# Bias tables of an attention block: reversed by TensorE, or loaded ready from repeated rows in DRAM

## The chip, the core and the metric

One NeuronCore of a Trainium2 chip runs the whole program; no other core takes part. The metric is the device time of one execution in microseconds (us). Engines are named TensorE (PE, with its weight load PEld), VectorE (DVE), ScalarE (ACT) and SyncE (SP), which here only issues DMAs. GpSimd does nothing.

## The reference

Two blocks in a row, for 256 tokens of width 1024, all in float32. The first has two layers; each is: a SwiGLU feed-forward (inner width 2816), a projection to three attention branches, the branches themselves, a gated merge, and a second feed-forward. The second block mixes attention and retention and ends in a mixture of experts; the change does not touch it. What matters here are the additive tables of the three branches:

```python
# neighbourhood branch, 8 heads, tokens on a grid of 4 rows x 64 columns
dr = row_idx - r[:, None] + (NA_WIN_ROWS - 1)
dc = jnp.clip(c[None, :] - c[:, None] + (NA_WIN_COLS - 1), 0, 2 * NA_WIN_COLS - 2)
bias = rpb[:, dr[:, None, :, None], dc[None, :, None, :]]
logits = jnp.where(col_ok[:, None, :], logits + bias, NEG_INF)
# differential and windowed branch, 4 + 8 heads
rel = kpos[None, :] - (start + qoff)[:, None]
bias = bias_table[t5_bucket(rel)]
```

Both tables depend only on key position minus query position. So each row of a table is the row above it, moved by one element. The neighbourhood table differs between the layers; the T5 table is the same for both.

## The kernel before, in words

**Weights.** All weights pass through a stream of pieces of 512 KB (`stream_plan`, `stream`), issued by SP in one fixed order into six buffers `W`. A piece i may be issued when piece i - 6 has been used up. Most pieces are split into two parts that TensorE multiplies at full rate: ScalarE rounds a piece to its high part (`halves`, L1324), VectorE subtracts to get the low part (`rests`, L1663), and four pairs of such parts (`WH`, `WL`) are kept. A product is then three matmuls. In one feed-forward, block b (of 11) takes two pieces for the gate, two for the up product and two for the down product of block b - 1, so 66 pieces in all; then the projection takes 30.

**Order.** Each engine runs its own list in order; semaphores tie them. TensorE's results go to four work banks of PSUM in turn (`begin`, `turns`), so a bank must be emptied four turns later. VectorE and ScalarE take the splits of the next pieces ahead of the emptying of a bank (`used`, then `take`), so a late piece holds both up.

**Bias rows.** Early in the first feed-forward the kernel makes the 112 padded rows of the neighbourhood bias (16 heads of both layers x 7 rows of 128) and 12 rows of 512 for T5, and stores them to the DRAM scratch `na_scr` and `t5_scr` (`store_bias_rows`). A DMA then reads a row once for each partition, one element further on each time (`load_t5` into `R5`, `load_na` and `load_na_bias` into `R`, which lies over `QK`). [...] TensorE turns it round by a product with the reversed identity `anti` (`bias`, recorded at L652 as reading R or QK, and C), and VectorE empties the bank into `T5` (L1810) or adds the column mask and writes `Z` (L1813). `bias_tables` deals three tables to each block from block 3 on: 12 + 8 in the first feed-forward of layer 0, 8 in that of layer 1. The loads of layer 0 stand in SP's stream at pieces 23, 28 and 33; those of layer 1 are issued by ScalarE between the norm and the second feed-forward of layer 0 (L1410).

**AdaLN units.** 24 products for the second block's modulation are dealt to chosen blocks (`ADA_BLOCKS`). Their weights have two buffers; the first four units use only the first of them, since `R5` takes the place of the other, and SP waits for the buffer ahead of a block's gate pieces (`load_ada`, L543).

## Time and profile before

| | us |
|---|---|
| runs, median (lowest to highest) | 2165.75 (2164.09 to 2170.45) |
| the profiled execution: its own time | 2166.41 |
| its span, from the first to the last instruction | 2164.6 |
| TensorE busy | 2062.4 |
| VectorE busy | 1181.1 |
| ScalarE busy | 637.2 |
| mean granted TensorE clock, share of full | 0.983 |

The profile is one execution; times in it count from the start of its span. A matmul's listed duration contains the depth of the pipeline, and matmuls overlap, so what one costs is the distance between starts. "Idle before" an instruction names what released it. SPq and ACTq are the DMA-issuing instructions of SP and ScalarE; a long one waited for room in its queue. q1 is SP's DMA queue, q10 ScalarE's. The names QK, T and t_scr in rows are the program's, numbers left out: T is `T5`, R is `R5`. The four feed-forwards start at about 18, 527, 731 and 1235 us.

### The profile page before, as it was taken

Reading aid. Unit: us, or ns where it says so; the run is one execution under the profiler, and the core shown is the slowest. Engines: PE = TensorE matmul, PEld = TensorE weight load, DVE = VectorE, ACT = ScalarE, POOL = GpSimd, SP = SyncE. Lnnn points to the kernel's source line nnn. Section 1 sums busy time; section 2 is a strip of 40 time slices with the busy share of each in tenths; the row PEclk is TensorE's granted clock in tenths of the full one; section 3 lists DMA queues with packets and bytes.
Section 4 is the critical chain, followed back from the end, with each engine's and each line's share of the span. In section 5 each row is a group of like instructions: output and inputs, shape, how many; then the busy total and the mean of one; then the engine's idle time right before and its main releaser. Section 6 shows DMA issues by size and latency. Waiting matters only on the chain.

```text
span 2164.6 us, 33353 instructions
## 1 busy us (share of the span) xinstructions
PE 2062.4 (95%) x14055; PEld 1676.9 (77%) x14055; DVE 1181.1 (55%) x2009; ACT 637.2 (29%) x942; POOL 0.2 (0%) x4
## 2 busy tenths in 40 slices
PE   7999999999999999999998999979997999999997
PEld 7999998878999999999886899978765543444443
DVE  6665659773656666565987365565275422222222
ACT  4433434432433533343443243320042000000001
POOL 0000000000000000000000000000000000000000
PEclk9999999999999999999999999999989999999999
DMA  7976563226966676556322677632224799999996
GB/s 226 276 218 178 164 184 98 88 88 193 282 216 201 200 225 216 176 158 185 103 92 78 195 243 215 195 73 78 79 97 175 315 422 420 421 421 421 421 421 252
DMA packets 260676, 471.39 MB, mean 218 GB/s; under 512 B 15418, under 2 KB 221300, under 8 KB 235948
## 3 DMA queue, kind: packets, MB, share of 16 engines
q1 hardware_dynamic: 259216, 466.25, 62.8%
q10 hardware_dynamic: 1308, 2.96, 0.6%
q8 instruction: 114, 1.87, 0.4%
q14 instruction: 38, 0.31, 0.0%
HBM read 468.03 MB, written 1.13 MB: 217 GB/s over the span
## 4 chain that ended last, share of the span: by engine, by line
PE 77%; DMA 17%; DVE 4%; ACT 1%; issue 1%; SPq 0%; DVEq 0%; ACTq 0%
PE ps L652 75%; DMA ring_zone<-in_moe_w_up_dram 15%; DMA W<-in_ffn_w_gate_dram 2%; PE ps L937 1%; DVE QK L1949 1%; PE ps L1082 0%; DVE hl L1674 0%; DVE WL L1663 0%; DVE xT L1681 0%; ACT WH L1324 0%; DMA PT<-in_norm_g_dram 0%; SPq L581 0%; DVE xT L1726 0%; DVE yT L1952 0%; DVE xT L1861 0%
## 5 line engine op out<-in xcount | busy, mean ns | idle before, releaser
L1663 DVE TENSOR_TENSOR WL<-W,WH 128x1024 fp32r<-128x1024 f32 x372 | 453.0, 1223 | 337.7 <-ACT WH L1324 337.7
L652 PE MATMUL ps<-hh,WH 128*128 128x256 f32 x2128 | 608.0, 286 | 13.4 <-DVE WL L1663 7.7
L652 PE MATMUL ps<-hl,WH 128*128 128x256 f32 x2128 | 598.1, 281 | 0.0
L652 PE MATMUL ps<-hh,WL 128*128 128x256 f32 x2128 | 597.9, 281 | 0.0
L1324 ACT ACTIVATE WH<-W 128x1024 fp32r<-128x1024 f32 x372 | 391.5, 1056 | 486.3 <-PE ps L652 455.9
L652 PEld LDWEIGHTS ps<-hh,WH 128*128 128x128 f32 x2128 | 404.0, 190 | 34.0 <-issue 31.1
L652 PEld LDWEIGHTS ps<-hl,WH 128*128 128x128 f32 x2128 | 404.1, 190 | 0.2
L652 PEld LDWEIGHTS ps<-hh,WL 128*128 128x128 f32 x2128 | 403.7, 190 | 0.0
L652 PE MATMUL ps<-ring_over,XT 128*64 128x512 f32 x896 | 228.4, 595 | 30.2 <-DMA ring_zone<-in_moe_w_up_dram 13.6
L652 PEld LDWEIGHTS ps<-ring_over,XT 128*64 128x64 f32 x896 | 77.7, 137 | 174.9 <-issue 174.5
L652 PE MATMUL ps<-hid_h,WH 128*128 128x256 f32 x704 | 201.7, 287 | 0.0
L652 PE MATMUL ps<-hid_l,WH 128*128 128x256 f32 x704 | 197.0, 280 | 0.0
L652 PE MATMUL ps<-hid_h,WL 128*128 128x256 f32 x704 | 196.8, 280 | 0.0
L1596 ACT ACTIVATE sgE<-ps 128x512 f32<-128x512 f32 x16 | 9.6, 597 | 447.5 <-PE ps L652 447.5
L652 PEld LDWEIGHTS ps<-hid_h,WH 128*128 128x128 f32 x704 | 132.6, 188 | 6.3 <-issue 5.8
L652 PEld LDWEIGHTS ps<-hid_l,WH 128*128 128x128 f32 x704 | 132.7, 188 | 0.5
L652 PEld LDWEIGHTS ps<-hid_h,WL 128*128 128x128 f32 x704 | 132.5, 188 | 0.0
L2379 DVE TENSOR_TENSOR hidE<-sgE,ps 128x512 f32<-128x512 f32 x16 | 16.8, 1048 | 205.0 <-PE ps L652 205.0
L652 PE MATMUL ps<-yT,W 128*128 128x256 f32 x512 | 116.7, 381 | 0.0
L652 PE MATMUL ps<-ring_zone,hidT 128*64 128x512 f32 x512 | 113.4, 595 | 0.8 <-DVE SelT L2361 0.7
L652 PEld LDWEIGHTS ps<-yT,W 128*128 128x128 f32 x512 | 95.0, 190 | 15.0 <-issue 3.6
L652 PEld LDWEIGHTS ps<-ring_zone,hidT 128*64 128x64 f32 x512 | 37.8, 137 | 65.4 <-issue 64.0
(336 smaller groups left out, 2343.5 us busy)
## 6 DMA issues: line engine op xcount, KB each, us to landing
ring_over<-in_moe_w_gate_dram SPq DMA_DIRECT2D x64, 1024.0 KB, 20.3
ring_zone<-in_moe_w_down_dram SPq DMA_DIRECT2D x64, 1024.0 KB, 18.9
ring_over<-in_moe_w_up_dram SPq DMA_DIRECT2D x48, 1024.0 KB, 22.3
W<-in_ffn_w_gate_dram SPq DMA_DIRECT2D x88, 512.0 KB, 5.2
W<-in_ffn_w_up_dram SPq DMA_DIRECT2D x88, 512.0 KB, 4.4
W<-in_ffn_w_down_dram SPq DMA_DIRECT2D x88, 512.0 KB, 4.2
W<-in_w_in_dram SPq DMA_DIRECT2D x78, 512.0 KB, 4.0
W<-in_w_gate_dram SPq DMA_DIRECT2D x48, 512.0 KB, 3.6
```

Source lines behind the costliest of these rows:

```text
L652: ins = nc.tensor.matmul(o, lhsT, rhs, start=start, stop=stop, skip_group_check=True, **kw)
L937: ins = nc.tensor.transpose(bank[:, k * T + q * P:k * T + (q + 1) * P], S[:, u % 4, q * T + k * P:q * T + (k + 1) * P], ident)
L1324: nc.scalar.activation(high, W[:, i % RAW, :], ACT.Copy).then_inc(high_ready, 1)
L1596: nc.scalar.activation(sgE[:, :], bank, ACT.Silu).then_inc(sg_ready, 1)
L1663: v.tensor_tensor(low, W[:, i % RAW, :], high.bitcast(F32), ALU.subtract).then_inc(low_ready, 1)
L1949: give(v.reciprocal(r2, r2))
L2379: v.tensor_tensor(hidE[:, :].rearrange("p (k m) -> p m k", k=HIDDEN), by_row(sgE[:, :]), by_row(bank), ALU.mult).then_inc(work_free, 2)
```

## The change

The rows go to DRAM scratch as before, and from there once more: each T5 row is copied 128 times in a row into `t5_rep` (12 x 128 x 512), each head's seven neighbourhood rows 64 times into `na_rep` (16 x 64 x 896), by two DMAs from DRAM to DRAM whose source repeats. In such a scratch a partition can read its own copy of the row one element further back than the partition before it (its start moves on by 511 or 895 elements), so the tables arrive in their right order: T5 straight in `T5` by one DMA of 128 x 12 runs of 1536 B, the neighbourhood table straight in `Z` by 16 DMAs (8 heads, two halves of 64 partitions) of 64 x 6 runs of 256 B each. The products, their work-bank turns and their evictions go; the column mask is added in place by VectorE during the projection (steps 2 to 9). SP issues the copies at pieces 36 and 42, waits for both before the T5 load at piece 50, and issues the 16 loads of layer 0 at piece 56; ScalarE issues the 16 of layer 1 where it issued two. VectorE waits for the T5 table ahead of the first projection, and for the neighbourhood table at its step 2. With `R` and `R5` gone, both adaLN buffers lie over `QK` and alternate from the first unit on.

The diff, cut (calls of `bias` and `bias_tables` in the engines' lists are left out):

```diff
@@ -28,7 +28,7 @@
-NA_RUN = 5 * P + 64
+NA_ROW = NA_ROWS * P
@@ -134,7 +133,7 @@
 def ada_buffer(u):
-    return 0 if u < ADA_ALONE else u % 2
+    return u % 2
 def ada_loads(u):
@@ -149,16 +148,8 @@
-STORE_AT, T5_AT, NA_AT = 20, 23, (28, 33)
-def bias_tables(l, i, b):
-    if i or not 3 <= b < FF_BLOCKS:
-        return []
-    tables = [("t5", h) for h in range(12)] + [("na", h) for h in range(NA_H)]
-    at = 3 * (b - 3)
-    return [t for t in tables[at:at + 3] if l == 0 or t[0] == "na"]
+STORE_AT, REPEAT_AT, T5_AT, NA_AT = 20, (36, 42), 50, 56
+NA_SHIFTS = 64
 def stream_plan():
@@ -304,12 +295,9 @@
-        _, R5, ada_a = zone(("V_and_QK", [P, TT * 1152 + 22 * T], F32), ("R5", [P, 12, 3 * P], F32),
-                            ("ada_a", [P, 2, PIECE], F32))
-        ada_b = zone(("up_to_ada_b", [P, TT * 1152 + 22 * T + 12 * 3 * P - 2 * PIECE], F32),
-                     ("ada_b", [P, 2, PIECE], F32))[1]
+        _, ada_a, ada_b = zone(("V_only", [P, TT * 1152], F32), ("ada_a", [P, 2, PIECE], F32),
+                               ("ada_b", [P, 2, PIECE], F32))
...
-        R5 = R5[:, :, :]
@@ -328,7 +316,6 @@
-        R = flat(QK[:, :, :]).rearrange("p (h n) -> p h n", h=NA_H)
@@ -371,6 +358,19 @@
+        na_rep = nc.dram_tensor("na_rep", (DEPTH * NA_H, NA_SHIFTS, NA_ROW), F32, kind="Internal").ap()
+        t5_rep = nc.dram_tensor("t5_rep", (12, P, 512), F32, kind="Internal").ap()
+        def load_na(queue, l):
+            for half in range(2):
+                first = l * NA_H * NA_SHIFTS * NA_ROW + (1 - half) * P + NA_SHIFTS - 1
+                for h in range(NA_H):
+                    src = bass.AP(tensor=na_rep.tensor, offset=first + h * NA_SHIFTS * NA_ROW,
+                                  ap=[[NA_ROW - 1, NA_SHIFTS], [P, 6], [1, 64]])
+                    queue.dma_start(Z[half * 64:half * 64 + 64, h, :].rearrange("p (a n) -> p a n", a=6), src)\
+                        .then_inc(r_load, 16)
@@ -598,16 +599,16 @@
                 sp.wait_ge(t5r, due(t5r))
...
+            def repeat_rows(scratch, rows, n):
+                return bass.AP(tensor=scratch.tensor, offset=0, ap=[[n, rows.shape[0]], [0, rows.shape[1]], [1, n]])
             def load_t5():
-                sp.wait_ge(scr, due(scr, 32))
-                src = bass.AP(tensor=t5_scr.tensor, offset=0, ap=[[1, P], [512, 12], [1, 3 * P]])
-                sp.dma_start(R5, src).then_inc(t5_load, 16)
-            def load_na(half):
-                src = bass.AP(tensor=na_scr.tensor, offset=half * P, ap=[[1, 64], [NA_ROWS * P, NA_H], [1, NA_RUN]])
-                sp.dma_start(R[half * 64:half * 64 + 64, :, :], src).then_inc(r_load, 16)
+                sp.wait_ge(repeated, 32)
+                sp.wait_ge(setup, 2)
+                src = bass.AP(tensor=t5_rep.tensor, offset=P - 1, ap=[[511, P], [P * 512, 12], [1, 3 * P]])
+                sp.dma_start(T5[:, :, :], src).then_inc(t5_load, 16)
             stream(0, RAW)
@@ -617,13 +618,16 @@
             stream(RAW, STORE_AT)
...
-            stream(STORE_AT, T5_AT)
+            stream(STORE_AT, REPEAT_AT[0])
+            sp.wait_ge(scr, due(scr, 32))
+            sp.dma_start(t5_rep, repeat_rows(t5_scr, t5_rep, 512)).then_inc(repeated, 16)
+            stream(REPEAT_AT[0], REPEAT_AT[1])
+            sp.dma_start(na_rep, repeat_rows(na_scr, na_rep, NA_ROW)).then_inc(repeated, 16)
+            stream(REPEAT_AT[1], T5_AT)
...
-            stream(T5_AT, NA_AT[0])
-            load_na(0)
-            stream(NA_AT[0], NA_AT[1])
-            load_na(1)
-            stream(NA_AT[1], moe_at)
+            stream(T5_AT, NA_AT)
+            load_na(sp, 0)
+            stream(NA_AT, moe_at)
...
             sp.wait_ge(table_ready, 1)
@@ -748,22 +752,6 @@
                 for tt in range(TT):
...
-            def bias(l, i, b):
-                for kind, h in bias_tables(l, i, b):
-                    if h == 0 and kind == "t5":
-                        pe.wait_ge(t5_load, 16)
-                    if h == 0 and kind == "na":
-                        pe.wait_ge(r_load, 32 * (l + 1))
-                    bank = begin()
-                    if kind == "t5":
-                        mm(bank[:, 0:384], anti, R5[:, h, :], True, True, then=work_ready)
-                    else:
-                        src = R[:, h, 0:640].rearrange("p (a n) -> p a n", n=P)[:, :, 0:64]
-                        mm(bank[:, 0:320], anti, src, True, True)
-                        mm(bank[:, 320:384], anti, R[:, h, 640:704], True, True, then=work_ready)
-                    turns.step()
             def norm():
@@ -1396,18 +1383,10 @@
                     if (l, i, b) == (0, 0, LATE_BLOCK):
...
-                    turns.step(len(bias_tables(l, i, b)))
                     if b:
...
-            def load_na_bias(l):
-                for half in range(2):
-                    first = (l * NA_H * NA_ROWS + half) * P
-                    src = bass.AP(tensor=na_scr.tensor, offset=first, ap=[[1, 64], [NA_ROWS * P, NA_H], [1, NA_RUN]])
-                    act.dma_start(R[half * 64:half * 64 + 64, :, :], src).then_inc(r_load, 16)
             def rows(tile, at, n, src):
@@ -1482,7 +1461,7 @@
                 if l + 1 < DEPTH:
-                    load_na_bias(l + 1)
+                    load_na(act, l + 1)
@@ -1802,16 +1781,13 @@
-            def bias(l, i, b):
-                for kind, h in bias_tables(l, i, b):
-                    bank = take()
-                    if kind == "t5":
-                        give(v.tensor_copy(T5[:, h, :], bank[:, 0:384]))
-                    else:
-                        mask = const("na_mask").rearrange("p (a n) -> p a n", a=1).to_broadcast([P, 6, 64])
-                        give(v.tensor_tensor(Z[:, h, :].rearrange("p (a n) -> p a n", a=6),
-                                             bank[:, 0:384].rearrange("p (a n) -> p a n", a=6), mask, ALU.add))
+            def mask_columns(l, h):
+                if h == 0:
+                    dve.wait_ge(r_load, 16 * 2 * NA_H * (l + 1))
+                mask = const("na_mask").rearrange("p (a n) -> p a n", a=1).to_broadcast([P, 6, 64])
+                z = Z[:, h, :].rearrange("p (a n) -> p a n", a=6)
+                return v.tensor_tensor(z, z, mask, ALU.add)
             def ffn(l, i):
                 for b in range(FF_BLOCKS):
@@ -1839,7 +1815,6 @@
                     if ada_unit(l, i, b - 1) is not None:
...
-                    bias(l, i, b)
                     if b:
...
                 if ada_unit(l, i, FF_BLOCKS - 1) is not None:
@@ -1868,7 +1843,11 @@
             for l in range(DEPTH):
...
+                if l == 0:
+                    dve.wait_ge(t5_load, 16)
                 for c in range(15):
+                    if 2 <= c < 2 + NA_H:
+                        link(mask_columns(l, c - 2))
                     if c != 1:
...
                     if c == 0:
```

## Rows read from the trace of the kernel before

**Rows 1.** page, parts 1 and 4: busy us; the chain by engine
```profile
PE 2062.4 (95%) x14055; PEld 1676.9 (77%) x14055; DVE 1181.1 (55%) x2009; ACT 637.2 (29%) x942; POOL 0.2 (0%) x4
...
PE 77%; DMA 17%; DVE 4%; ACT 1%; issue 1%; SPq 0%; DVEq 0%; ACTq 0%
```

**Rows 2.** timeline of TensorE, blocks 3 and 7: start us, us, engine, line, operation
```profile
77.43 0.29 PE L652 MATMUL ps<-hh,WL 128*128 128x256 f32 x1
77.55 2.10 PE L652 MATMUL ps<-R,C 128*128 128x384 f32 x6
...
79.61 0.28 PE L652 MATMUL ps<-hid_l,WH 128*128 128x256 f32 x1
...
158.05 2.48 PE L652 MATMUL ps<-QK,C 128*128 128x320 f32 x12
...
160.53 0.28 PE L652 MATMUL ps<-hid_l,WH 128*128 128x256 f32 x1
```

**Rows 3.** waits, whole span: us in total, times, longest
```profile
ACT WH L1324 <- PE ps L652: 455.9, 248, 5.4
```

**Rows 4.** timeline of TensorE, block 5, in brackets the idle time before
```profile
116.74 1.54 PE L652 MATMUL ps<-R,C 128*128 128x384 f32 x4
120.20 0.91 PE L652 MATMUL ps<-R,C 128*128 128x384 f32 x2 [1.92 <-DVE S L1827]
```

**Rows 5.** the chain in order of time, 60 to 235 us
```profile
100.86 16.35 DMA W<-in_ffn_w_gate_dram
```

**Rows 6.** waits of SP's own queue, 90 to 101 us
```profile
SPq L543 <- PE ps L652: 4.0, 1, 4.0
```

**Rows 7.** waits of TensorE, 520 to 600 us
```profile
PE ps L652 <- DVE WL L1663: 2.1, 2, 1.2
```

**Rows 8.** groups by line: busy us, mean ns of one | idle before
```profile
L1813 DVE TENSOR_TENSOR Z<-ps,C 128x384 f32<-128x384 f32 x16 | 8.0, 549 | 0.1
```

**Rows 9.** windows, projection: busy us by engine, PEclk, DMA share, GB/s
```profile
250.00:270.00 20.00, 20.00 (x171) 19.86 (x170) 13.49 (x17) 6.92 (x8) 0.00 (x0) 1.00 0.63 184
```

**Rows 10.** timeline of SP: pieces 36 and 37, pieces 56 and 57
```profile
110.36 4.14 SPq L581 DMA_DIRECT2D W<-in_ffn_w_up_dram  x2
...
171.54 4.21 SPq L581 DMA_DIRECT2D W<-in_ffn_w_down_dram  x2
```

**Rows 11.** DMA issues, whole span: KB each, median us to landing
```profile
W<-in_ffn_w_gate_dram SPq DMA_DIRECT2D x88, 512.0 KB, 5.2
...
R<-t_scr SPq DMA_DIRECT2D x1, 2304.0 KB, 14.1
```

**Rows 12.** windows: small packets; loads into 64 partitions beside weights
```profile
18.50:21.00 2.50, 2.50 (x15) 2.50 (x15) 1.23 (x1) 0.00 (x0) 0.00 (x0) 0.61 1.21 84
...
80.00:94.00 14.00, 14.00 (x122) 14.00 (x121) 8.78 (x17) 5.69 (x6) 0.00 (x0) 1.00 1.06 260
```

**Rows 13.** DMA packets, 18.5 to 21 us, then 72 to 76 us
```profile
DMA packets 2376, 0.21 MB, mean 84 GB/s; under 512 B 2341, under 2 KB 2372, under 8 KB 2376
...
DMA packets 1103, 1.48 MB, mean 370 GB/s; under 512 B 15, under 2 KB 1102, under 8 KB 1102
```

**Rows 14.** timeline of ScalarE and its queue at the loads of layer 1
```profile
528.62 0.73 ACTq L1410 DMA_DIRECT2D QK<-na_scr  x1
...
529.42 2.18 ACT L1343 ACTIVATE mT<-xT 128x512 f32<-128x512 f32 x4
531.50 1.99 ACT L1324 ACTIVATE WH<-W 128x1024 fp32r<-128x1024 f32 x2
```

**Rows 15.** timeline of TensorE, second feed-forward, start of the up product
```profile
534.38 0.38 PE L652 MATMUL ps<-hh,WH 128*128 128x256 f32 x1
```

**Rows 16.** timeline of SP, one weight piece
```profile
535.24 9.44 SPq L581 DMA_DIRECT2D W<-in_ffn_w_gate_dram  x1
```

**Rows 17.** DMA queues, 530 to 543 us: packets, MB, share of 16 engines
```profile
q10 hardware_dynamic: 655, 1.80, 58.2%
q1 hardware_dynamic: 1530, 1.66, 48.8%
```

More of the change, by code:

```diff
@@ L122 @@
               ((1, 1), (1, 3, 4, 6, 7, 9)))
-ADA_ALONE = 4
 ADA_UNITS = {}
@@ L419, in build @@
         scr = ev("scratch_written")
+        repeated = ev("scratch_repeated")
         r_load = ev("shifted_load")
@@ L1841, in ffn @@
                         ada_columns(ada_unit(l, i, b - 1))
-                    bias(l, i, b)
                     if b:
```

## The prediction

> **What bounds the kernel now.** Read first the busy shares and the chain of waits [rows 1]: TensorE is busy for 95% of the span and carries 77% of the chain; the DMA share of 17% belongs almost wholly to the expert stage, which the change doesn't touch. So in the feed-forward stages an instruction taken off TensorE should shorten the span by what it held TensorE for, and VectorE (55%) and ScalarE (29%) count only where they make TensorE wait. Next the order of TensorE's instructions around the bias products [rows 2]: an ordinary product (listed at 0.29 us, which is pipeline depth) is followed 0.12 us after its start, so cost has to be read from starts, not from durations. Then the two places in these stages where TensorE stood still [rows 4, 7] and what was late there. Last the rates of the DMA engines and how two queues share them [rows 12, 13, 17], because the change trades products for transfers.
>
> **Removed: 28 bias products.** In block 3 of the first feed-forward the step before the products starts at 77.43, the three T5 products at 77.55, and the second ordinary product after them at 79.61; without them it would start at 77.67. Three T5 products (the six instructions of the row) cost 1.94 us, and the twelve of them stand in four blocks: 7.8 us. Three neighbourhood products (twelve instructions) run from 158.05, and the second ordinary product starts at 160.53 where 158.17 would do: 2.36 us, 0.79 each. There are 16, eight in each layer: 12.6 us. Together 20.4 us off TensorE, and nothing lies beside them: over the kernel ScalarE waits 455.9 us for TensorE before its roundings, 248 times [rows 3], so the work on weights follows TensorE and not the other way round.
>
> **Removed: two stalls.** The first is inside block 5: the third product starts at 120.20, after a wait of 1.92 us, where 116.74 and two thirds of 1.94 make 118.03, so 2.2 us are lost [rows 4]. Its chain is a weight piece issued at 100.86 that took 16.35 us to land behind two skewed neighbourhood loads [rows 5]; SP had also stood 4.0 us for the single adaLN buffer before it [rows 6]. From the moment the piece could have gone to its landing is 16.35 + 4.0 + 1 for the adaLN issues, some 21 us, and 2.2 us of that reached TensorE. So some 19 us of lateness of a piece are covered: this is the cover I use below. Both causes go: the loads move, and the first four adaLN units now alternate. The second stall is 2.1 us at 558 to 564 [rows 7], a piece late behind the second layer's loads (2.9 MB). They become 1.6 MB. I take both as gone, unless something of the new takes their place: 4.3 us.
>
> **Moved on VectorE.** 28 evictions leave the feed-forward, and 16 mask additions, which took 0.55 us each out of PSUM [rows 8], enter the input projection, reading SBUF now. There VectorE is busy 13.5 of 20 us while TensorE is busy for all 20 [rows 9], so an addition of about that length in each of 8 steps hides. Bounds: 0 to 16 x 0.6 = 10 us if each held up an eviction that TensorE waits for; I take 0.3, by the idle third. The new wait for the T5 table stands at the end of the stage; its load is issued 16 pieces before that end. A piece takes 3.06 us (piece 36 at 110.36, piece 56 at 171.54 [rows 10]), so 49 us earlier, and the load took 14.1 us in its old form [rows 11]. The neighbourhood table is issued 10 pieces before the end and wanted two projection steps of some 5.6 us after it, 42 us in all. Neither is late; queued behind these waits on VectorE would be the low halves of all weights.
>
> **Added: two copies from DRAM to DRAM**, 3.1 MB and 3.7 MB, on SP's queue at pieces 36 and 42, that is about 107 and 125 us [rows 10]. The trace of before shows no such transfer. At the saturated rate of 370 GB/s [rows 13] they take 8.5 and 10 us; if a byte read and written in DRAM counts twice, 17 and 20. A piece behind them lands that much after its usual 5.2 us [rows 11]. Against 19 us of cover the first case costs 0, the second 3 + 6 = 9 us. I take 1, since loads into SBUF run at that rate and the copies lie 18 us apart. SP's wait for both comes at piece 50, about 150 us: 25 us after the second, hidden in the first case, some us late in the second (in the 9).
>
> **Added: the tables' own loads.** The T5 load is the same 2.3 MB as before. The neighbourhood table becomes 16 transfers of 384 runs of 256 B, 6144 runs for a layer, instead of 2 of 512 long ones. Price of a run: between 18.5 and 21 us the engines moved 2376 packets, 2341 of them under 512 B, in 2.5 us, the engines full (share 1.21) [rows 12, 13]: 1.05 ns each over 16 engines, so 6.5 us. From above, packets of 1.3 KB took 4 us for 1103 [rows 13], 3.6 ns each, so 22 us. I take 1.5 ns, near the row with packets of their size.
>
> In layer 0, SP issues them at piece 56, about 170 us. An issue took up to 0.73 us on ScalarE for 512 runs [rows 14], so SP is held 16 times that at most, 12 us, and the piece behind lands inside the 19 us. At 3.6 ns it would be 22 + 5.2 - 19 = 8.5 us late. I take 1.
>
> In layer 1, ScalarE issues them, and this is the dear place. At 528.6 it issues two now; the four squares already handed over run until 531.6, and the next weight piece is rounded at 531.50 [rows 14]. Queued behind the sixteen issues are these roundings (with the low halves on VectorE behind them), the sum's copy and the square root. TensorE has three pieces in hand and starts the up projection at 534.38 [rows 15]; the fourth piece is needed 24 products later, at 537.2. Rounding (1.06), low half (1.22) and handshakes take 2.4 us, so ScalarE must be free by 534.8, 6.2 us after the first issue. Sixteen issues at 0.73 with nothing else end at 540.3: 5.5 us lost. At half that, nothing. A queue also fills: with five pieces of 512 runs ahead, one issue took 9.44 us [rows 16], so about 2560 runs fit and 3584 must drain first, in half of the engines' time, as the two queues share them now (58% and 49%) [rows 17]. At 1.05 ns that is 7.5 us (1.3 lost), at 1.5 ns 10.8 (4.6), at 3.6 ns 25.8 (19.6). I take 6.
>
> The Trainium skill (DMA: Bandwidth & Descriptors, Specifications) has a rule against this change: under 512 B a DMA engine reads, modifies and writes, so full rate needs at least that. If a run of 256 B costs like one of 512 B, a layer's table takes 8.5 us at 370 GB/s, 1.4 ns a run, close to what the small-packet row allows; the sum would not move.
>
> **Sum**, against the profiled execution (2166.4 us, its span 2164.6): -20.4 - 4.3 + 0.3 + 1 + 1 + 6 = -16.4, so 2150.0. That execution lies 0.7 us above the median of the three runs (2165.75), inside their spread (2164.09 to 2170.45); I say 2150.
>
> **The rivals.**
> *A, part of the gain comes back in the small loads*, 2 to 3 ns a run: ScalarE is held 14 to 21 us (8 to 15 lost), SP's piece is late by 0 to 5, the copies take 1 to 2. With the 25 us gained: 2153 to 2163, say 2160. For it: loads into 64 partitions ran at 260 GB/s [rows 12] where others ran at 370 [rows 13], and the new ones write 64 partitions too. Against: the packets of their size were cheap.
> *B, slower than before.* The same mechanism with its upper price at each place: 19.6 on ScalarE, 8.5 on SP, 9 at the copies, 0.3 on VectorE, against 24.7: +12.7, 2179. With p the price of a run in ns and 2 us for the copies, the loss is (7.17p - 6.2) + (6.14p - 13.8) + 2, and passes 24.7 at p = 3.2. That needs small packets to cost three times what they did at 20 us.
> *C, the products were hidden anyway*, so that the blocks are paced by the splitting of weights and only the stalls go: about 2164. Against it stand ScalarE's waits for TensorE [rows 3] and the gapless starts around the products [rows 2].
> *D, everything is covered*: ScalarE is free in time and nothing is late: 2166.4 - 24.7 = 2142.
>
> **Chances.** Forecast 0.62 (its own range 2145 to 2156), A 0.15, B 0.08, C 0.05, D 0.10. What a measurement can tell from no change is 0.3%, 6.5 us, so the line is 2159.3: faster 0.62 + 0.10 + half of A = 0.80; within it half of A and C, 0.12; slower 0.08. The range 2142 to 2163 leaves out B and edges of C and D.
>
> **What would show it.** TensorE: no rows from the reversing matrix, and each block with three of them shorter by 1.9 to 2.4 us; the layer-1 gap at 534 to 540, released by the low half of a weight, of about 6 us; no gap at 118 or 560. ScalarE: sixteen issues of 0.4 to 0.8 us each; if later ones take over 1 us, the queue filled and A is at work. SP: an idle stretch before the T5 load means that the copies were dear. The forecast is wrong if the blocks do not shorten by these amounts, if TensorE stands still in the first layer between 110 and 200 us for over 3 us, or if VectorE waits for a table.

## The result, and the profile after

| | before | after |
|---|---|---|
| runs, median (lowest to highest), us | 2166.04 (2164.09 to 2170.45) | 2148.09 (2148.00 to 2150.22) |
| ratio, 95% interval | | 0.9917 (0.9899 to 0.9934) |
| span of the profiled execution, us | 2164.6 | 2148.4 |

Faster by 0.8%, where 2150 was forecast. In a later session, beside other runs of before, the same kernel stood at 0.9937 (0.9918 to 0.9956).

The page of the kernel after, parts 1, 2 and 4: busy us by engine, packets of the DMA engines, the chain by engine, to be held against [rows 1].

```profile
PE 2042.2 (95%) x13967; PEld 1660.9 (77%) x13967; DVE 1175.9 (55%) x1997; ACT 637.0 (30%) x942; POOL 0.2 (0%) x4
...
DMA packets 273951, 475.57 MB, mean 221 GB/s; under 512 B 28182, under 2 KB 234064, under 8 KB 249224
...
PE 78%; DMA 15%; DVE 4%; ACT 1%; ACTq 1%; issue 0%; SPq 0%; DVEq 0%
```

TensorE lost 88 instructions and 20.2 us of busy time, which are the 28 groups of products. The chain lost two points of DMA (the late pieces), and ACTq, ScalarE's DMA issues, rose in it from 0% to 1%. The gain by stage is read best from windows that are cut at the same instructions in every kernel, at VectorE's `hl` in the norms that stand before and behind a feed-forward; FFN(l,i) is feed-forward i of layer l. The columns are the window, its length, busy us by engine, PEclk, DMA share, GB/s. Before: attention of layer 0, FFN(0,1), FFN(1,0).

```profile
230.19:528.49 298.30, 291.57 (x1929) 255.76 (x1930) 202.46 (x388) 110.86 (x216) 0.00 (x0) 0.99 0.42 128
528.49:729.33 200.84, 197.84 (x1737) 191.50 (x1735) 122.94 (x145) 82.41 (x89) 0.00 (x0) 1.00 0.78 234
729.33:935.98 206.65, 204.74 (x1774) 197.29 (x1774) 128.46 (x158) 84.21 (x94) 0.00 (x0) 1.00 0.65 199
```

The same stages of the kernel after.

```profile
214.62:513.01 298.39, 291.66 (x1929) 255.54 (x1930) 206.35 (x395) 110.86 (x216) 0.00 (x0) 0.99 0.42 129
513.01:721.21 208.20, 199.64 (x1737) 193.45 (x1735) 122.91 (x144) 82.15 (x89) 0.00 (x0) 0.98 0.76 219
721.21:921.65 200.44, 198.54 (x1742) 192.38 (x1742) 124.64 (x149) 84.25 (x94) 0.00 (x0) 1.00 0.68 205
```

FFN(0,0) ends at 214.62 instead of 230.19: 15.6 us gained. Attention is unchanged. FFN(0,1) is 7.4 us longer. FFN(1,0) is 6.2 us shorter. Behind it 1.8 us are gained (1228.6 to 1226.8), where the change only adds the mask additions of layer 1: 1.6 of them fall in layer 1's projection and attention, whose first 20 us ran at a granted clock of 0.91 before and 1.00 after. Windows of 2 us at the same place, 4.0 us into that stage, before and then after:

```profile
939.98:941.98 2.00, 2.00 (x11) 2.00 (x11) 0.45 (x2) 2.00 (x5) 0.00 (x0) 0.50 0.00 0
```

```profile
925.65:927.65 2.00, 2.00 (x20) 2.00 (x19) 0.46 (x2) 2.00 (x5) 0.00 (x0) 1.00 0.04 8
```

In both, TensorE had stopped for the same 1.54 us in the norm ahead of them. All stages together give -16.2, as the spans do.

The loss is one gap. TensorE and ScalarE of the kernel after around it (start us, us, operation, in brackets the idle time before):

```profile
529.62 0.58 PE L656 MATMUL ps<-hh,WH 128*128 128x256 f32 x1 [7.65 <-DVE WL L1642]
```

```profile
513.14 0.73 ACTq L371 DMA_DIRECT2D Z<-na_rep  x1
...
515.99 11.15 ACTq L371 DMA_DIRECT2D Z<-na_rep  x12
527.25 2.95 ACT L1311 ACTIVATE WH<-W 128x1024 fp32r<-128x1024 f32 x3 [11.13 <-issue]
```

From the first issue at 513.14 to the end of the last at 527.15 ScalarE was held for 14.0 us, and the next weight piece could be rounded only then. The chain of waits shows the single issues; these are four of them, from 517 to 523 us (start us, us, what):

```profile
517.63 2.03 ACTq L371
...
519.69 0.65 ACTq L371
...
520.37 2.04 ACTq L371
...
522.44 0.65 ACTq L371
```

Two of the sixteen took 2.0 us and one 0.91; the last seven took 0.65 each. And the gap costs more than its length. Windows of the kernel after behind it: PEclk is the third column from the right.

```profile
525.00:529.00 4.00, 0.00 (x0) 0.00 (x0) 0.66 (x1) 1.75 (x2) 0.00 (x0) 0.67 1.40 153
529.00:531.00 2.00, 1.38 (x6) 1.38 (x7) 2.00 (x3) 1.91 (x3) 0.00 (x0) 0.50 0.92 121
531.00:533.00 2.00, 2.00 (x12) 2.00 (x11) 1.97 (x2) 1.91 (x3) 0.00 (x0) 0.50 0.88 310
533.00:535.00 2.00, 2.00 (x16) 1.95 (x16) 0.00 (x0) 0.23 (x1) 0.00 (x0) 0.95 1.08 370
```

For the first 3.6 us after the gap TensorE ran at half of full clock (1.2 instead of 2.4 GHz), a matmul every 0.21 us instead of every 0.12: some 1.7 us more. The Trainium skill (TensorE: Matmul & The Clock Gate, Part 1) says that an idle array falls back to the lower of its two clocks; the trace agrees, 0.50 behind an idle stretch of 7.65 us.

### The profile page after: what moved, and what is told of

It reads as the page before. It is cut to its first block, busy times and chain, and to the rows that moved or that the text cites. A ratio compares the mean times of both kernels' runs of the same rounds, so it can differ in the third digit from the quotient of the medians.

```text
span 2148.4 us, 33210 instructions
## 1 busy us (share of the span) xinstructions
PE 2042.2 (95%) x13967; PEld 1660.9 (77%) x13967; DVE 1175.9 (55%) x1997; ACT 637.0 (30%) x942; POOL 0.2 (0%) x4
## 4 chain that ended last, share of the span: by engine, by line
PE 78%; DMA 15%; DVE 4%; ACT 1%; ACTq 1%; issue 0%; SPq 0%; DVEq 0%
PE ps L656 77%; DMA ring_zone<-in_moe_w_up_dram 15%; PE ps L924 1%; DVE QK L1928 1%; ACTq L371 1%; PE ps L1069 0%; DVE hl L1653 0%; DVE xT L1660 0%; DVE WL L1642 0%; DMA PT<-in_norm_g_dram 0%; SPq L582 0%; ACT WH L1311 0%; DVE xT L1705 0%; DVE yT L1931 0%; DVE xT L1836 0%
## 6 DMA issues: line engine op xcount, KB each, us to landing
ring_over<-in_moe_w_gate_dram SPq DMA_DIRECT2D x64, 1024.0 KB, 20.4
```

## The experiments

All stage times are those windows. "Wait" is TensorE's wait behind ScalarE's issues in FFN(0,1), "hold" the time from ScalarE's first such issue to the end of its last.

| kernel | median us | ratio to before (95%) | FFN(0,0) ends | FFN(0,1) | FFN(1,0) | hold | wait |
|---|---|---|---|---|---|---|---|
| before | 2162.4 to 2166.0 | 1 | 230.19 | 200.84 | 206.65 | | |
| after | 2148.09 | 0.9917 (0.9899 to 0.9934) | 214.62 | 208.20 | 200.44 | 14.0 | 7.65 |
| after, again | 2148.08 | 0.9937 (0.9918 to 0.9956) | 213.23 | 210.00 | 200.44 | 15.0 | 8.6 |
| loads issued by SP | 2139.31 | 0.9888 (0.9868 to 0.9907) | 215.12 | 198.25 | 201.99 | 0 | 0 |
| the same, again | 2139.89 | 0.9897 (0.9881 to 0.9912) | 213.36 | 198.30 | 202.02 | 0 | 0 |
| eight each | 2140.67 | 0.9905 (0.9888 to 0.9923) | 213.12 | 199.65 | 200.44 | 7.5 | 1.1 |
| 16 issues of 64 runs | 2145.61 | 0.9912 (0.9891 to 0.9932) | 213.88 | 204.03 | 200.46 | 10.3 | 4.0 |
| 12 issues of 512 runs | 2148.29 | 0.9929 (0.9908 to 0.9949) | 213.65 | 208.26 | 200.45 | 14.4 | 8.0 |
| no mask additions | 2148.78 | 0.9931 (0.9912 to 0.995) | 214.22 | 210.74 | 200.45 | 16.7 | 10.3 |
| one adaLN buffer | 2151.1 | 0.9933 (0.9913 to 0.9953) | 215.52 | 208.85 | 200.45 | 15.3 | 8.9 |
| copies twice | 2169.8 | 1.0032 (1.0014 to 1.005) | 235.30 | 208.94 | 200.44 | 15.4 | 9.0 |
| before, no products | 2145.1 | 0.9918 (0.9896 to 0.9939) | 219.03 | 200.04 | 200.44 | | |
| before, loads later | 2163.9 | 0.9989 (0.9976 to 1.0003) | 228.12 | 200.79 | 206.66 | | |
| before, both | 2146.0 | 0.9931 (0.9912 to 0.995) | 214.26 | 201.52 | 200.45 | | |

The kernel before ran beside each group of experiments again, so its median has a range. The ratios are uncertain by some 0.2%, 4 us, so the verdicts rest on stages of one profiled execution each. These don't all repeat equally well:

- FFN(1,0) does: 200.44 to 200.46 in ten profiles without the products.
- "FFN(0,0) ends" contains the first 43 us, which hold none of the loads, copies or products in question and yet differ by up to 2.0 us: VectorE's eleventh low half starts at 42.0 to 44.0. From that instruction to the end of the stage it is 187.6 us before, 171.6 and 171.1 in the two profiles of the kernel after. Below this is called the count from 43 us; it resolves 0.5 us.
- The hold does not. Where ScalarE issues all sixteen loads unchanged, it is 14.0, 15.0, 15.3, 15.4 and 16.7 us in five profiles, and FFN(0,1) takes 208.2 to 210.7 us with it.

**1. SP issues layer 1's loads.** The same sixteen loads move from ScalarE's program into SP's stream, ahead of a gate piece of block 6.

```diff
+                    if plan[i] == ("ffn_gate", (0, 1), 6, 0):
+                        load_na(sp, 1)
...
-                if l + 1 < DEPTH:
-                    load_na(act, l + 1)
```

> From the kernel after: the sixteen neighbourhood loads of layer 1 leave ScalarE's program and stand in SP's stream, ahead of the gate piece of block 6, first half, of FFN(0,1). Theory (ScalarE's sixteen issues hold it 12.6 us and TensorE waits 7.65 us for it, then runs about 1.9 us longer at a granted clock of 0.50): both go, 2148.1 - 7.65 - 1.9 = 2138.5 us, ratio to before 0.987. Rival 1 (the clock would have dipped there in any case, only the wait goes): 2140.4 us. Rival 2 (SP holds its weight pieces up as long as ScalarE was held, because the price is in the queue and not in the engine): the pieces of block 6 come late, TensorE waits there up to 7 us, and the time stays at 2145 to 2148 us.

It came out as the first theory has it: 2139.3 us, no wait behind a late piece, FFN(0,1) 198.25 us instead of 208.20, 9.9 us where the theory's 7.65 + 1.9 is 9.6. The same 2 us of window that ran at half clock before are at full clock here:

```profile
529.00:531.00 2.00, 2.00 (x19) 2.00 (x18) 1.79 (x4) 0.76 (x3) 0.00 (x0) 1.00 0.92 302
```

FFN(1,0) is 1.6 us longer in both profiles of this kernel than elsewhere; its first 20 us ran at a granted clock of 0.91, and why is not known. The second rival falls too. SP needed 11.3 us for the sixteen, about as long an issue as ScalarE's, and the piece behind was late by that, but no instruction of TensorE waited for it. The edit changes the engine and also the moment, some 75 us later; that it is ScalarE's hold that counted rests on experiments 2 to 4. In the timeline of SP, second run of this kernel:

```profile
587.23 11.26 SPq L371 DMA_DIRECT2D Z<-na_rep  x16
598.53 1.16 SPq L584 DMA_DIRECT2D W<-in_ffn_w_gate_dram  x2
```

**2. The price of an issue, against the price of a run.** One segment of six for each load of layer 1.

```diff
+            segments = 1 if l else 6
...
-                                  ap=[[NA_ROW - 1, NA_SHIFTS], [P, 6], [1, 64]])
+                                  ap=[[NA_ROW - 1, NA_SHIFTS], [P, segments], [1, 64]])
```

> From the kernel after: each of ScalarE's sixteen loads of layer 1 brings one of its six segments (64 runs of 256 B instead of 384; 1024 runs in all instead of 6144). The remaining five sixths of the layer-1 neighbourhood table are left as they were, so that part of the table is not computed. Theory A (each issue costs ScalarE about 0.65 us whatever it carries; only the two issues of about 2.03 us are the queue being full): ScalarE is held 16 x 0.65 = 10.4 us, TensorE waits 7.65 - (12.6 - 10.4) = 5.4 us, and the time is 2148.1 - 2.2 = 2145.9 us. Theory B (the prediction's: ScalarE is held by runs, 6.2 us after the first issue at 1.5 ns a run once the queue holds its fill): with 1024 runs nothing fills the queue, the issues take what ScalarE's single issues took before, the wait goes, and the time is 2139 to 2141 us.

With a sixth of the runs ScalarE was still held for 10.3 us; the last twelve issues took 0.62 us each, the first four 0.50 to 0.72 us. From the chain of waits of this kernel, two of the twelve:

```profile
515.65 0.62 ACTq L374
...
522.12 0.62 ACTq L374
```

So theory A holds: three quarters of the hold of 14.0 us are the sixteen instructions themselves and hardly depend on the data (0.62 us with 64 runs, 0.65 with 384). The wait fell by 3.7 us, not by 2.2, because the hold had been counted from the third issue (12.6) instead of the first (14.0).

**3. Fewer, larger loads.** The same 6144 runs in twelve issues.

```diff
+                if l:
+                    for a in range(6):
+                        src = bass.AP(tensor=na_rep.tensor, offset=first + a * P,
+                                      ap=[[NA_ROW - 1, NA_SHIFTS], [NA_SHIFTS * NA_ROW, NA_H], [1, 64]])
+                        queue.dma_start(Z[half * 64:half * 64 + 64, :, a * 64:(a + 1) * 64], src).then_inc(r_load, 16)
+                    continue
...
```

> From the kernel after: the same 6144 runs of layer 1 are loaded by twelve instructions of 512 runs (one for each half and segment, over all eight heads) instead of sixteen of 384. Theory A (a price for each issue): the hold falls by 4 x 0.65 = 2.6 us, TensorE waits 5.0 us, time 2145.5 us. Theory B (a price for each run): nothing changes, 2148.1 us. Theory C (the price of an issue grows with its runs, 0.65 us for 384, so 0.87 us for 512): 12 x 0.87 = 10.4 us as before plus the same two blocked issues, 2148.1 us, with issues near 0.87 us in the trace.

Hold 14.4, wait 8.0: the 2.6 us that theory A takes off did not come off the kernel after's first profile (14.0), but against all five profiles with sixteen issues (14.0 to 16.7) the 14.4 is inside the scatter. So this run can't choose between theories B and C, and it shows A's sum of issues alone to be short of the hold. From the chain of waits of this kernel:

```profile
515.79 1.92 ACTq L372
...
517.74 2.97 ACTq L372
...
522.38 0.66 ACTq L372
...
523.83 0.98 ACTq L372
```

The hold thus has two parts. Each issue takes 0.65 us (0.64 to 0.98 in the eight short ones with 512 runs, 0.75 in the mean, half way to theory C's 0.87), and in the middle some issues take up to 2.97 us, as one of SP's took 9.44 before [rows 16]. What happens in the middle is to be seen in the queues of the kernel after, from the first issue to 522.44 us, and from there to the end of the last issue (packets, MB, share of 16 engines):

```profile
q1 hardware_dynamic: 1853, 2.22, 84.0%
q10 hardware_dynamic: 1564, 0.39, 21.5%
```

```profile
q10 hardware_dynamic: 3158, 0.78, 138.9%
```

While weight pieces that SP had issued before were still landing, ScalarE's queue moved only some 1500 runs (0.39 MB) in 9.3 us. When they were through, it moved some 3050 in 4.7 us, 1.5 ns each, and no issue took over 0.65 us any more. At the end of an issue at most some 1960 runs were issued and not yet landed here, 1930 in experiment 4, 2080 with 512 runs an issue. That the long issues waited for room fits this, but it is not all: in the kernel without mask additions the third issue took 1.49 us with 768 runs ahead of it.

```profile
514.14 1.49 ACTq L371 DMA_DIRECT2D Z<-na_rep  x1
```

How these waits would go down with the load on the other queue was not varied.

**4. Eight each.** ScalarE issues the first eight, SP the rest where experiment 1 had them.

```diff
-        def load_na(queue, l):
+        def load_na(queue, l, halves=(0, 1)):
...
+                    if plan[i] == ("ffn_gate", (0, 1), 6, 0):
+                        load_na(sp, 1, (1,))
...
-                    load_na(act, l + 1)
+                    load_na(act, l + 1, (0,))
```

> From the kernel after: ScalarE issues only the first eight of its sixteen loads of layer 1, where it issued them before; SP issues the other eight ahead of the gate piece of block 6 of FFN(0,1). Theory (TensorE's wait is ScalarE's hold less 6.4 us: 14.0 - 6.4 = 7.65 in the kernel after, 10.3 - 6.3 = 4.0 with 64 runs, 14.4 - 6.4 = 8.0 with twelve issues, 16.7 - 6.4 = 10.3 without the mask): eight issues at 0.65 us hold it 5.2 us, 7 us if the queue fills at the last of them, so TensorE waits 0 to 0.8 us, the clock does not fall and FFN(0,1) takes 198 to 199.5 us against 208.2; time about 2139 us. Rival (each issue on ScalarE costs TensorE its share, 7.65 / 16 = 0.48 us): a wait of 3.8 us, FFN(0,1) 203 us, time 2143.5 us.

The hold was 7.5 us, with one issue of 1.18 and one of 1.96 us, so the wait by the rule is 1.1, and it was 1.1, a little more than the 0 to 0.8 expected from a hold of at most 7 (waits of TensorE, 500 to 600 us):

```profile
PE ps L658 <- DVE WL L1644: 1.1, 1, 1.1
```

Wait = hold - 6.4 holds to 0.1 us for all eight holds of the table, from 7.5 with a wait of 1.1 to 16.7 with one of 10.3. The rival's 3.8 is out.

**5. The mask additions.** VectorE's sixteen instructions are left out.

```diff
-                    if 2 <= c < 2 + NA_H:
-                        link(mask_columns(l, c - 2))
+                    if c == 2:
+                        dve.wait_ge(r_load, 16 * 2 * NA_H * (l + 1))
```

> From the kernel after: VectorE's sixteen mask additions are left out, so the neighbourhood tables lack the column mask. Theory (prediction's term +0.3: VectorE has the room, 28 of 40 us busy in the stretch): no change, 2147.8 to 2148.1 us. Rival (the 16 additions stand in the chain between TensorE's projection and its banks, 0.45 us each): 2148.1 - 7 = 2141 us.

The additions cost nothing in their own stage. The windows over the same 40 us of the projection, the kernel after first:

```profile
234.62:274.62 40.00, 40.00 (x341) 39.98 (x342) 27.88 (x33) 14.87 (x14) 0.00 (x0) 1.00 0.69 194
```

```profile
234.62:274.62 40.00, 40.00 (x343) 39.99 (x343) 23.84 (x27) 14.95 (x15) 0.00 (x0) 1.00 0.67 197
```

VectorE is busy 4.0 us less, TensorE for all 40 us in both, and attention takes 298.39 and 298.36 us. Behind FFN(1,0), where layer 1's additions lie, it is 1226.8 and 1226.7 us. FFN(0,1) is 2.5 us longer in this profile with its hold of 16.7 us, the largest of the five, and no mask addition stands in that stage.

**6. The kernel before without its products.** TensorE's `bias` goes, and VectorE sets the tables to zero in their place; all loads stay.

```diff
-                    bias(l, i, b)
...
-                    bank = take()
-                    if kind == "t5":
-                        give(v.tensor_copy(T5[:, h, :], bank[:, 0:384]))
...
+                    link(v.memset((T5 if kind == "t5" else Z)[:, h, :], 0.0))
```

> From the kernel before: the 28 groups of bias products on TensorE and their evictions are left out, everything that loads the skewed tables stays. VectorE sets the tables to zero at the same places, so the biases are not computed. Theory (the products are on the path at their full length, 20.4 us): FFN(0,0) gets 14.1 us shorter, FFN(1,0) 6.3 us, the two stalls stay (2.2 us in block 5, 2.1 us at 558 to 564), time 2163.0 - 20.4 = 2142.6 us, ratio 0.9906. Rival C of the prediction (the products fill time in which TensorE would wait for pieces anyway): the weight pieces become the bound in FFN(0,0), the stall in block 5 grows by what the products took until then (up to 4 us), and the time stays at 2147 us or above.

FFN(1,0) is 6.2 us shorter, as in the kernel after. FFN(0,0) gives only 11.2 of 14.1 us by its end and 11.9 in the count from 43 us. The median, 2145.1 us (2141.6 to 2160.2), lies between the theory's 2142.6 and the rival's 2147. The chain and TensorE's waits between 80 and 140 us:

```profile
90.90 10.45 DMA W<-in_ffn_w_down_dram
101.35 17.03 DMA W<-in_ffn_w_gate_dram
```

```profile
PE ps L652 <- DVE WL L1661: 3.3, 2, 2.2
```

The skewed loads still made pieces late, and a TensorE that is ahead by the products of two blocks meets them sooner: it waits 3.3 us where it waited 1.9 [rows 4]. So the products did hide something, by 2.2 us.

**7. The kernel before with its loads apart.**

```diff
-STORE_AT, T5_AT, NA_AT = 20, 23, (28, 33)
+STORE_AT, T5_AT, NA_AT = 20, 23, (31, 40)
```

> From the kernel before: its two skewed neighbourhood loads of layer 0 move from pieces 28 and 33 to pieces 31 and 40, so that they don't lie together in front of a piece that block 5 needs. Nothing else is changed, the products stay. Theory (the stall of 2.2 us in block 5 is caused by these two loads together): it goes, time 2163.0 - 2.2 = 2160.8 us, FFN(0,0) ends 2.2 us earlier, provided that the tables are there when the products of block 5 and 6 want them. Rival (the stall is the single adaLN buffer's): it stays, 2163.0 us.

The chain of waits runs through the whole of FFN(0,0) on TensorE, where it broke at 100.86 [rows 5], and the stage ends 2.07 us earlier, 2.5 us shorter in the count from 43 us:

```profile
43.07 181.46 PE ps L652 x1507
```

Its total (0.9989, 0.9976 to 1.0003) can't be told from no change, as 2.2 us is below what the runs resolve. The end of the stage alone could not show it either, since the same kernel's ends differ by 1.4 us; that the wait is gone from the chain does. The single adaLN buffer is still there in this kernel.

**8. Both: no products, loads apart.**

> From the kernel without products (its biases are zero): its two skewed neighbourhood loads of layer 0 move from pieces 28 and 33 to 31 and 40, as in the kernel in which they alone were moved. Theory (with the products gone and those loads in place the lateness that the products had covered came out as 3.3 us of waits, so that only 11.2 of 14.1 us were gained; each part alone is worth 2.1 and 11.2 us, together more): FFN(0,0) ends 14.1 + 2.1 = 16.2 us before the kernel before's 230.2, at 214.0, with no wait for a piece, time 2163.9 - 20.4 - 2.1 = 2141 us or less. Rival (pieces are late wherever the loads stand, once TensorE is faster): it ends at 216 to 219 and the time is as without the move, 2142 to 2145 us.

FFN(0,0) ends at 214.26, no waits for a piece between 80 and 140 us. In the count from 43 us the two edits are worth 11.9 and 2.5 us alone and 16.5 together; with the loads apart the products are worth 14.0 of the 14.1 forecast. The profiled execution took 2143.1 us where 2141 or less was expected; the median of 2146.0 (2143.1 to 2151.0) is further off, and what made the other runs longer isn't known, as only one is profiled.

**9. The adaLN buffer.** The first four units use one buffer again.

```diff
-    return u % 2
+    return 0 if u < 4 else u % 2
```

> From the kernel after: the first four adaLN units share one buffer again instead of two. SP waits for that buffer as before the change (4.0 us ahead of one piece). Theory (the two causes of the stall in block 5 were the skewed loads and this wait; with the loads gone the 19 us cover the wait): 2148 us, no wait of TensorE in FFN(0,0). Rival (the second buffer is what removed the stall): TensorE waits 2 us in block 5 and the time is 2150 us.

SP waits again, and TensorE doesn't. Waits of SP's queue, 85 to 125 us, and the chain of this kernel:

```profile
SPq L544 <- PE ps L656: 3.0, 1, 3.0
```

```profile
43.95 167.99 PE ps L656 x1451
```

FFN(0,0) ends 0.9 us later only because it began 0.9 later: the count from 43 us is 171.6 in both. The total, 0.9933, is that of the kernel after's second set of runs (0.9937). So the second buffer brought nothing once the skewed loads were gone, and experiment 7 lost the stall with the single buffer in place: the stall needed the skewed loads. Whether they made it alone, without the wait for the buffer, was not run.

**10. The copies twice.** Each copy from DRAM to DRAM is preceded by one into a spare tensor.

```diff
+            sp.dma_start(t5_more, repeat_rows(t5_scr, t5_more, 512)).then_inc(more, 16)
             sp.dma_start(t5_rep, repeat_rows(t5_scr, t5_rep, 512)).then_inc(repeated, 16)
...
+            sp.dma_start(na_more, repeat_rows(na_scr, na_more, NA_ROW)).then_inc(more, 16)
             sp.dma_start(na_rep, repeat_rows(na_scr, na_rep, NA_ROW)).then_inc(repeated, 16)
```

> From the kernel after: each of the two copies from DRAM to DRAM is preceded by one of the same size into a spare tensor, on the same queue (3.1 MB and 3.7 MB more). Theory (a piece may be some 19 us late before TensorE sees it): the piece behind the first pair lands 14.4 + 10 = 24 us after its issue, 5 us beyond its usual 5.2 + 19 or nothing, the one behind the second pair 16.9 + 12 = 29 us, with the first lateness not made up by then some 5 to 10 us beyond it; time 2148 + 5 to 10 = 2153 to 2158 us, waits of TensorE at 120 to 150 us for a piece of weights. Rival (the copies run beside the pieces and the ring is deeper than 19 us): no wait, 2148 us. Rival (copies slow each other, so that doubling costs more than twice): above 2163 us.

TensorE waited twice, 4.9 and 10.5 us, as the first theory has it; but the stage lost 20.7 us (20.1 in the count from 43 us) and the kernel 21, where 5 to 10 were expected. The total, 2169.8, lies where the second rival puts it, and its reason is not borne out: from the issue of the first copy to the landing of the piece behind it 27.5 us passed instead of 16.4, at the second pair 33.2 instead of 18.5, about twice the lateness for twice the bytes. Waits of TensorE between 60 and 212 us, and two windows behind the first wait:

```profile
PE ps L662 <- DVE WL L1648: 15.4, 2, 10.5
```

```profile
130.00:132.00 2.00, 1.77 (x8) 1.80 (x9) 1.68 (x3) 1.38 (x2) 0.00 (x0) 0.50 1.10 371
132.00:134.00 2.00, 2.00 (x12) 2.00 (x11) 1.46 (x2) 0.51 (x1) 0.00 (x0) 0.50 1.03 410
```

Of the remaining 4.7 to 5.3 us most is the clock, at half for 4.5 to 4.7 us behind each wait. The piece that the first wait was for could go at about 101.7 (as in the kernel after) and landed at 127.75: 26.1 us, of which 4.9 reached TensorE, so 21 were covered, where the forecast worked with 19.

**Sessions side by side.** The kernel after and that of experiment 1 ran once more beside each other.

> The kernel after once more, beside the kernel below and the kernel before on one chip, so that the two can be compared directly: ratio to before 0.991 to 0.993, TensorE's wait behind ScalarE's issues 7.6 to 10.3 us, as in the runs so far.

> The kernel whose layer-1 loads are issued by SP, once more: ratio to before 0.987 to 0.989, and 8 to 10 us below the kernel after.

2148.08 against 2139.89: the version with SP's issues is 8.2 us faster than the kernel after, and 22 to 24 us faster than the one before. With eight issues each (2140.7) it can't be told apart. The runs of the kernel after spread from 2141.9 to 2153.8 here, so the 8.2 is rough; FFN(0,1) is 11.7 us shorter.

## Why the prediction came out right

Its number held to 2 us, but several of its terms were off in ways that cancelled. Against the kernel before on the same runs the gain was 18.0 us in the first set and 14.3 in the second, for 16.4 forecast.

- **Products.** 20.4 us off TensorE was right: TensorE's busy time fell by 20.2, and layer 1's part came out at 6.21 for 6.3. For layer 0 the sentence "nothing lies beside them" was right only with the loads moved: experiment 6 gets 11.9 for 14.1, experiment 8 the full amount. Products and stall had to be summed as a pair, and the change happened to remove both. Rival C, all hidden, is out; a sixth of it was true of layer 0.
- **Stalls.** The first, 2.2 us: 2.1 to 2.5 by experiment 7. Of the two causes named it needed the skewed loads; SP's 4.0 us for the buffer [rows 6] made no wait without them. The second, 2.1 us, went: without ScalarE's hold FFN(0,1) takes 198.3 us for 200.8.
- **Copies, +1, and SP's loads in layer 0, +1.** Both cost nothing that a stage shows; FFN(0,0) gained 15.6, and 16.0 and 16.5 in the count from 43 us, where 16.3 less 2 was forecast. Experiment 8, which has no copies and the old loads, takes the same 171.1 us. In the kernel after, the two copies and the sixteen issues, timeline of SP:

```profile
99.63 0.88 SPq L623 DMA_DIRECT2D t_rep<-t_scr  x1
...
117.39 1.10 SPq L625 DMA_DIRECT2D na_rep<-na_scr  x1
...
157.37 13.15 SPq L371 DMA_DIRECT2D Z<-na_rep  x16
```

  and the first landing behind each copy, from the DMA issues of 101.6 to 101.9 and of 117.3 to 119.2 us (KB each, us to landing):

```profile
W<-in_ffn_w_up_dram SPq DMA_DIRECT2D x1, 512.0 KB, 14.4
```

```profile
W<-in_ffn_w_up_dram SPq DMA_DIRECT2D x1, 512.0 KB, 16.9
```

  The forecast of the cheap case was 5.2 + 8.5 = 13.7 and 5.2 + 10 = 15.2. A byte read and written in DRAM did not count twice, and 19 to 21 us of cover took the lateness, as experiment 10 shows by exceeding it.
- **VectorE, +0.3.** Nothing, by experiment 5.
- **ScalarE in layer 1, +6.** The mis-sized term. It was the dear place, and "ScalarE must be free 6.2 us after the first issue" was right to 0.2 us (6.4 in eight profiles). What failed is the hold: "sixteen issues at 0.73 with nothing else" and the draining queue were taken as two alternatives, of which the longer counts, and gave 10.8 to 11.7. They came one after the other: 3.6 us of long issues while the weight pieces held the engines, then issues at their own price of 0.65 us with nothing to wait for, 10.4 + 3.6 = 14.0. The price of a run was right, 1.5 ns for a forecast 1.5, once q10 had the engines to itself; "half of the engines' time" was not, 21.5% over the first 9.3 us, and no more than some 2080 runs ever stood in its queue, not 2560. And I priced the wait at its length, without the clock behind it. Wait and clock together are 9.9 us against experiment 1's second run (208.20 less 198.30), 11.7 in the second run of the kernel after.
- **What cancelled.** FFN(0,1) came out 3.5 us worse than forecast (+7.4 for +3.9), FFN(0,0) 1.3 us better, and the stretch behind FFN(1,0) 1.8 us better by its clock. So 2150.0 for a profiled 2150.22 owes something to luck; the forecast's own range, 2145 to 2156, is the fairer measure.
- **Rivals.** A and B rested on the price of a run, 2 to 3 ns and above 3.2. It was 1.5, and experiment 2 shows that most of the hold was no price of runs at all. Yet the sign of A, issues of over 1 us, did appear, and in layer 1 the hold of 14.0 us and the wait of 7.65 stand at and just below the lower edge of A's figures (14 to 21, 8 to 15); A's total failed because nothing came back at SP and the copies. D, everything covered, did not come about in the change as made, but experiment 1 is D: it would take 24.7 us off, and 22.5 and 23.7 were measured.

## What to carry to other kernels

A DMA issue is an instruction of the engine that issues it: sixteen small loads on an engine that also rounds every weight piece hold the pieces up by sixteen times 0.65 us, with 64 runs almost as with 384, so put them on the engine that only issues, or count them against the time until that engine is wanted. Look what is still landing from the other queue when the issues begin: waits for it come on top of the issue time, and the larger of the two is not the sum. When work on the bounding engine is removed, look again at the transfers that were just in time, and price a wait of TensorE with the clock behind it: here 4.0 us cost 5.7, and 7.65 cost 9.9. In the kernel before each partition reads one element further on than the one above it, in the kernel after one element further back; a load that reads one row of scratch with falling addresses, which would need neither products nor copies, was not tried.

## What the runs showed of the hardware

- The two waits of experiment 6, 1.1 and 2.2 us, left the granted clock at 1.00; so did the 1.1 us of experiment 4; the waits of 4.0 us and more were followed by 3 to 5.5 us at 0.50, and FFN(0,1) lost 1.6 to 3.1 us beyond the wait in seven profiles. The length of a wait does not settle it: behind the same stop of 1.54 us in the norm at the end of a stage the granted clock was 0.50 in the kernel before and 1.00 in the kernel after, as the two windows at 939.98 and 925.65 show.
- An issue of a DMA took ScalarE 0.62 us with 64 runs, 0.65 with 384 and 0.64 to 0.98 with 512, and SP 0.70 (11.26 for sixteen) to 0.82 (13.15). The Trainium skill (DMA: Bandwidth & Descriptors, Issuing engines are not separate DMA queues) calls the time to initiate a DMA usually small beside the DMA. Here it was 0.65 us against landings of 6.2 us in the median, small for each, and yet it was the cost, since sixteen stood in a row.
- Stretches that the change doesn't touch differ by their clock. From the end of FFN(1,0) to the end of the span it is 1226.8 us in the kernel after and 1221.9 in its second profile, with the same instructions. Two windows of the first, then of the second:

```profile
1421.65:1471.65 50.00, 39.92 (x189) 33.07 (x189) 28.62 (x48) 8.37 (x15) 0.00 (x0) 0.86 0.14 43
1621.65:1671.65 50.00, 39.76 (x207) 30.14 (x208) 27.46 (x90) 11.45 (x21) 0.00 (x0) 0.86 0.46 179
```

```profile
1422.01:1472.01 50.00, 39.92 (x201) 33.48 (x200) 30.19 (x49) 8.37 (x15) 0.00 (x0) 0.90 0.14 43
1622.01:1672.01 50.00, 39.11 (x211) 26.97 (x211) 28.00 (x107) 12.06 (x22) 0.00 (x0) 0.90 0.47 179
```

  So a term of 2 us can be shown by a stage, and not by the total of one execution.
